# A relative bias tile read back skewed from sixteen copies in DRAM, and a score block taken in front of a chunk's split

## The reference

```python
def t5_bucket(dist):
    d = jnp.maximum(dist, 0)
    large = 16 + (log(max(d, 1) / 16) / log(8) * 16).astype(int32)   # at most 31
    return jnp.where(d < 16, d, large)

# selected and window branches (8 heads), for query t and key s:
s_w = einsum(qb, kb) * scale + head_bias[:, :, t5_bucket(t - s)]
# compressed branch: block n ends at position 16 n + 31, 15 blocks
s_c = einsum(qb, kc) * scale + head_bias[:, :, t5_bucket(t - (16 * n + 31))]
# sliding window of 128 with sinks (4 more heads)
s = einsum(q, k) * scale + head_bias_swa[:, :, t5_bucket(t - s)]
```

## Time and profile before

| | |
|---|---|
| median of three runs | 2382.7 us |
| the profiled execution, its span | 2386.48 us, 2384.7 us |
| mean granted TensorE clock | 0.982 of full speed |
| TensorE busy | 2305.5 us, 97% |
| VectorE busy | 1540.0 us, 65% |
| ScalarE busy | 1187.1 us, 50% |
| GpSimd busy | 66.7 us, 3% |
| DMA, mean over the span | 206 GB/s |

### The profile page before, as it was taken

How to read it: one execution, slowest core, us unless ns; L and a number is a source line. 1 busy time by engine, 2 the same in 40 slices (tenths; PEclk the granted TensorE clock), 3 DMA queues, 4 the chain that set the end, 5 groups by cost and what they waited for, 6 DMA issues and landing times.

```text
span 2384.7 us, 34244 instructions
## 1 busy us (share of the span) xinstructions
PE 2305.5 (97%) x14956; PEld 2068.2 (87%) x14956; DVE 1540.0 (65%) x1425; ACT 1187.1 (50%) x1156; POOL 66.7 (3%) x84
## 2 busy tenths in 40 slices
PE   8999999999999999999999999999999999799998
PEld 8997989799899888897998999778888898688886
DVE  4654655666466547556664666668888566588887
ACT  3433544443343346344433544467776554377774
POOL 1000100000000001000000000000000100000000
PEclk8999999999999999999999999999999999799999
DMA  6554434455555554444655555489998554499995
GB/s 207 182 190 159 144 121 145 153 168 189 183 176 178 193 167 131 141 128 151 196 188 174 177 177 187 143 288 355 357 349 301 174 186 149 143 335 347 343 370 191
DMA packets 309613, 490.92 MB, mean 206 GB/s; under 512 B 15349, under 2 KB 204965, under 8 KB 309457
## 3 DMA queue, kind: packets, MB, share of 16 engines
q1 hardware_dynamic: 305696, 475.35, 59.3%
q0 software_dynamic: 2912, 10.14, 1.3%
q10 hardware_dynamic: 848, 3.15, 0.4%
HBM read 487.53 MB, written 1.07 MB: 205 GB/s over the span
## 4 chain that ended last, share of the span: by engine, by line
PE 90%; DVE 5%; ACT 2%; issue 1%; POOL 0%; DMA 0%; DVEq 0%; ACTq 0%
PE PS L682 27%; PE PS L686 26%; PE PS L683 26%; PE PS L1338 1%; ACT RH L1449 1%; PE PS L904 1%; PE PS L869 1%; DVE RL L1932 1%; PE PS L854 1%; PE PS L1268 1%; DVE HTL L1918 1%; PE PS L1344 1%; DVE X L2273 1%; PE PS L843 1%; PE PS L805 0%
## 5 line engine op out<-in xcount | busy, mean ns | idle before, releaser
L1932 DVE TENSOR_TENSOR RL<-RINGS,RH 128x2048 fp32r<-128x2048 f32 x448 | 1017.6, 2273 | 552.4 <-ACT RH L1449 550.0
L1449 ACT ACTIVATE RH<-RINGS 128x2048 fp32r<-128x2048 f32 x448 | 851.3, 1901 | 787.4 <-PE PS L686 787.1
L682 PE MATMUL PS<-RH,HTH 128*128 128x256 f32 (+1 forms) x1728 | 565.2, 338 | 4.7 <-DVE HTL L1918 2.6
L683 PE MATMUL PS<-RH,HTL 128*128 128x256 f32 (+1 forms) x1728 | 553.3, 331 | 0.0
L682 PE MATMUL PS<-HTH,RH 128*128 128x256 f32 (+1 forms) x1568 | 416.9, 285 | 12.2 <-ACT RH L1449 5.0
L683 PE MATMUL PS<-HTL,RH 128*128 128x256 f32 (+1 forms) x1568 | 413.3, 282 | 0.0
L686 PE MATMUL PS<-RL,HTH 128*128 128x256 f32 (+1 forms) x1728 | 408.1, 328 | 0.0
L682 PEld LDWEIGHTS PS<-RH,HTH 128*128 128x128 f32 x1728 | 330.4, 191 | 40.1 <-issue 5.8
L683 PEld LDWEIGHTS PS<-RH,HTL 128*128 128x128 f32 x1728 | 331.5, 192 | 29.0 <-issue 0.2
L686 PE MATMUL PS<-HTH,RL 128*128 128x256 f32 (+1 forms) x1568 | 329.6, 283 | 1.4 <-DVE RL L1932 1.4
L686 PEld LDWEIGHTS PS<-RL,HTH 128*128 128x128 f32 x1728 | 296.9, 191 | 31.4
(11 more groups left out here) (413 smaller groups left out, 2282.1 us busy)
## 6 DMA issues: line engine op xcount, KB each, us to landing
RINGS<-w_in SPq DMA_DIRECT2D x64, 1024.0 KB, 5.3
RINGS<-w_gate SPq DMA_DIRECT2D x64, 1024.0 KB, 5.4
RINGS<-w_up SPq DMA_DIRECT2D x64, 1024.0 KB, 5.5
RINGS<-w_down SPq DMA_DIRECT2D x64, 1024.0 KB, 5.4
RINGS<-ffn_w_gate SPq DMA_DIRECT2D x44, 1024.0 KB, 5.4
RINGS<-ffn_w_up SPq DMA_DIRECT2D x44, 1024.0 KB, 5.3
RINGS<-ffn_w_down SPq DMA_DIRECT2D x44, 1024.0 KB, 4.9
RINGS<-w_out SPq DMA_DIRECT2D x16, 1024.0 KB, 5.0
```

What stands on the lines that cost most here:

```text
L682: mm(dst, a_[0], b_[0], start=start, stop=False)
L683: mm(dst, a_[0], b_[1], start=False, stop=False) if left else mm(dst, a_[1], b_[0], start=False, stop=False)
L1449: A(splits.buffer(RH, RH3)[:, 0:width], RINGS[:, slot, 0:width], ACT.Copy).then_inc(wh_ready, 1)
L1932: TTn(RL[:, slot, 0:width], RINGS[:, slot, 0:width], splits.buffer(RH, RH3)[:, 0:width].bitcast(F32), ALU.subtract).then_inc(wl_ready, 1)
```

## The change

The one row per head stays. GpSimd now stores it sixteen times in DRAM, as (16, 12, 512). Eight DMAs then read it back, each to 16 partitions. Within one DMA partition p reads from copy p with a shift of p elements back, which gives the right order of partitions at once, directly into BIAS. The flip matmuls, the reversed identity, the matrix HOT with its load, and the 30 matmuls for BIASC go. VectorE adds the masks in place in BIAS, behind the last chunk pair of the first FFN, and in projection step 2 copies every sixteenth element of BIAS into BIASC; blocks that the first 128 rows never see come from the mask. In both layers `softmax(0)` and `blocks(0)` move from the start of step 9 to the end of step 8, in front of that step's `split`, and `blocks(0)` stands between the addition and the maximum of `softmax(0)`.

```diff
-NLOAD = 6
+NLOAD = 5
+COPIES = 16
@@ gpsimd
-            nc.gpsimd.dma_start(HOT, hot).then_inc(consts_loaded, 16)
...
-                    nc.gpsimd.dma_start(scratch, VBIAS).then_inc(bias_stored, 16)
+                    nc.gpsimd.dma_start(scratch.rearrange("r h n -> h r n"), spread(VBIAS, 1, COPIES)).then_inc(bias_stored, 16)
                     pool.wait_ge(bias_stored, 16)
-                    nc.gpsimd.dma_start(BFLIP, bass.AP(tensor=scratch.tensor, offset=P, ap=[[1, P], [512, 12], [1, S]])).then_inc(bias_loaded, 16)
+
+                    for q in range(0, P, COPIES):
+                        nc.gpsimd.dma_start(BIAS[q:q + COPIES, :, :], bass.AP(tensor=scratch.tensor, offset=S - 1 - q,
+                                                                              ap=[[12 * 512 - 1, COPIES], [512, 12], [1, S]])).then_inc(bias_loaded, 16)
@@ tensor
-                    if l + f == 0 and j == 1:
-                        for t in range(T):
-                            for n in range(NCMP):
-                                u = t * P - 16 * n - 31 + 256
-                                last = mm(PS[:, 6, (t * NCMP + n) * 8:(t * NCMP + n + 1) * 8], HOT[:, u:u + P], RB[:, 0:8], start=True, stop=True)
-                        last.then_inc(hot_ready, 1)
                 if l + f == 0:
-                    pe.wait_ge(bias_taken, 4)
+                    pe.wait_ge(bias_row, 1)
...
-                    if l == 0 and j == 0:
-                        pe.wait_ge(bias_loaded, 16)
-                        for b in range(6):
-                            last = mm(PS[:, 4 + b if b < 4 else b - 2, :], CON[:, O_FLIP:O_FLIP + P], BFLIP[:, 2 * b:2 * b + 2, :].rearrange("p h n -> p (h n)"), start=True, stop=True)
-                        last.then_inc(hot_ready, 1)
                     if j == 2:
-                        if l == 0:
-                            pe.wait_ge(bias_taken, 6)
@@ vector, swiglu
+                if l + f == 0:
+                    dve.wait_ge(bias_loaded, 16 * (P // COPIES))
+                    TTn(BIAS[:, 0:8, :], BIAS[:, 0:8, :], spread(CON[:, O_MB:O_MB + S], 1, 8), ALU.add).then_inc(bias_taken, 1)
+                    TTn(BIAS[:, 8:12, :], BIAS[:, 8:12, :], spread(CON[:, O_MS:O_MS + S], 1, 4), ALU.add).then_inc(bias_taken, 1)
                 for j in range(FR - 2):
                     split()
@@ vector, softmax
                     TTn(p.rearrange("p (g j n) -> p g j n", g=2, n=nk), PS[:, 2:4, 0:nj * nk].rearrange("p g (j n) -> p g j n", n=nk),
                         bias, ALU.add).then_inc(sc_taken, 1)
+                    if between is not None:
+                        between()
@@ vector, projection
+                    if l == 0 and i == 2:
                         dve.wait_ge(zeroed, 4)
-                        dve.wait_ge(bias_taken, 6)
+                        dve.wait_ge(bias_taken, 2)
+                        for t in range(T):
+                            seen = 7 if t == 0 else NCMP
+                            first = P + 31 - t * P
+                            for r in range(2):
+                                own = BIASC[:, r * 8 + t * 4:r * 8 + t * 4 + 4, :]
+                                V.tensor_copy(own[:, :, 0:seen].rearrange("p (g i) n -> p g i n", g=2),
+                                              BIAS[:, 0:8, first:first + 16 * seen - 15:16].rearrange("p (g r i) n -> p r g i n", g=2, r=2)[:, r]).then_inc(bias_taken, 1)
+                                if seen < NCMP:
+                                    V.tensor_copy(own[:, :, seen:NCMP], spread(CON[:, O_MCN + seen:O_MCN + NCMP], 1, 4)).then_inc(bias_taken, 1)
+                        dve.wait_ge(bias_taken, 8)
...
                     if i == 9:
-                        softmax(0)
-                        dve.wait_ge(pads_zeroed, l + 1)
-                        dve.wait_ge(ktr_ready, 2 * l + 1)
-                        blocks(0)
                         dve.wait_ge(head_sq, 2 * l + 2)
...
+                    if i == 8:
+
+                        def first_blocks():
+                            dve.wait_ge(pads_zeroed, l + 1)
+                            dve.wait_ge(ktr_ready, 2 * l + 1)
+                            blocks(0)
+
+                        softmax(0, first_blocks)
                     if i <= 10 or i >= 16:
                         split(K * W1[i + 2] if i + 2 < N1 else SLOT)
```

More of the change, by code:

```diff
@@ L206, in loop, with build @@
         c.after(m, count, per)
-def build(nc, a, out, con, hot_rev, hot, vect, scratch):
+def build(nc, a, out, con, hot_rev, vect, scratch):
     ctx = ExitStack()
@@ L290, in build @@
         BT = BTF.rearrange("p (a r n) -> p a r n", a=2, r=16)
-        BFLIP = TT[:, 0:12, :]
-        HOTR, HOT, VBIAS = (TT[0:n, 12 + 2 * i:14 + 2 * i, :].rearrange("p a n -> p (a n)") for i, n in enumerate((32, 32, 12)))
+        HOTR, VBIAS = (TT[0:n, 12 + 2 * i:14 + 2 * i, :].rearrange("p a n -> p (a n)") for i, n in enumerate((32, 12)))
         DIAG = TT[:, 18, :].rearrange("p (t n) -> p t n", t=T)
@@ L1987, in swiglu @@
                         V.tensor_copy(VBIAS, PS[0:12, 5, :]).then_inc(bias_row, 1)
-                    if l + f == 0 and j == 1:
-                        dve.wait_ge(hot_ready, 2)
-                        for t in range(T):
-                            for r in range(2):
-                                TTn(BIASC[:, r * 8 + t * 4:r * 8 + t * 4 + 4, :].rearrange("p (g i) n -> p g i n", g=2),
-                                    PS[:, 6, t * NCMP * 8:(t + 1) * NCMP * 8].rearrange("p (n g r i) -> p r g i n", g=2, r=2, i=2)[:, r],
-                                    spread(spread(CON[:, O_MCN + t * NCMP:O_MCN + (t + 1) * NCMP], 1, 2), 1, 2), ALU.add).then_inc(bias_taken, 1)
+                if l + f == 0:
+                    dve.wait_ge(bias_loaded, 16 * (P // COPIES))
+                    TTn(BIAS[:, 0:8, :], BIAS[:, 0:8, :], spread(CON[:, O_MB:O_MB + S], 1, 8), ALU.add).then_inc(bias_taken, 1)
+                    TTn(BIAS[:, 8:12, :], BIAS[:, 8:12, :], spread(CON[:, O_MS:O_MS + S], 1, 4), ALU.add).then_inc(bias_taken, 1)
                 for j in range(FR - 2):
@@ L2026, in _, with softmax @@
                 heads = PROJ[:, :, NG:NG + 24]
-                def softmax(u):
+                def softmax(u, between=None):
                     kind, t, j0, nj = UNITS[u]
@@ L2101, in _ @@
                         outputs(i - 12)
-                    if l == 0 and i == 1:
-                        dve.wait_ge(hot_ready, 3)
-                        TTn(BIAS[:, 0:8, :], HIGH.rearrange("p (h n) -> p h n", h=8), spread(CON[:, O_MB:O_MB + S], 1, 8), ALU.add).then_inc(bias_taken, 1)
-                        TTn(BIAS[:, 8:12, :], LOW[:, 4 * S:8 * S].rearrange("p (h n) -> p h n", h=4), spread(CON[:, O_MS:O_MS + S], 1, 4), ALU.add).then_inc(bias_taken, 1)
+                    if l == 0 and i == 2:
                         dve.wait_ge(zeroed, 4)
-                        dve.wait_ge(bias_taken, 6)
+                        dve.wait_ge(bias_taken, 2)
[9 more added lines that the diff above has]
+                        dve.wait_ge(bias_taken, 8)
                     if i == 3:
@@ L2670, in constants @@
     hot_rev = (t5_bucket(383 - w) == b).astype(np.float32)
-    hot = (t5_bucket(w - 256) == b).astype(np.float32)
-    return con, hot_rev, hot
+    return con, hot_rev
 def input_order():
@@ L2711 @@
     arrays = {n: np.ascontiguousarray(x) for n, x in inputs.items()}
-    for n, x in zip(("con", "hot_rev", "hot"), constants()):
+    for n, x in zip(("con", "hot_rev"), constants()):
         arrays[n] = x
@@ L2717 @@
     out = nc.dram_tensor("out", (1, S, D), F32, kind="ExternalOutput").ap()
-    scratch = nc.dram_tensor("bias_scratch", (12, 512), F32, kind="Internal").ap()
-    build(nc, aps, out, aps["con"], aps["hot_rev"], aps["hot"], aps["vect"], scratch)
+    scratch = nc.dram_tensor("bias_scratch", (COPIES, 12, 512), F32, kind="Internal").ap()
+    build(nc, aps, out, aps["con"], aps["hot_rev"], aps["vect"], scratch)
     r = run(nc, [arrays], core_ids=[0])
```

7 lines of the change are left out of this document (3 added, 4 removed).

## The result

The changed kernel takes 2367.2 us (median of five runs, 2364.41 to 2373.23) against 2382.7 us before on the same chip: 0.9936 of it, with an interval of 0.9917 to 0.9955. That is 15.5 us faster; the forecast was 18.4 us faster, 2364.3 us, with a range of 2358 to 2370.

What follows compares the result with a forecast made beforehand. TensorE, busy 97% of the span, was taken to bound the kernel. Terms 13.3 + 5.15 + 0 + 0 - 0.1 = 18.4 us, taken from 2382.7, gave 2364.3 us; own range 2361.5 to 2367, wider 2358 to 2370.

Steps and rivals of the forecast that it cites:

- A: First FFN: removing the 60 matmuls for BIASC gives 13.3 us, 10.7 of it matmuls and about 2.5 clock.
- B: Projection, between chunks 0 and 1: removing the six flip matmuls gives 5.15 us, bounds 4.5 and 5.15.
- C: VectorE's new bias additions and six small copies into BIASC fall into its idle time; cost 0, at most 1.3 us.
- D: The 16-fold store and eight reads beside the ring loads in the first FFN: between 0 and 3 us, taken as 0.
- R3: Rival: the eight DMAs are so slow that VectorE waits for them and the kernel gets slower; chance 0.02.
- E: Moved scores and blocks, both layers: scores(2) 4.3 us earlier together, less 4.4 for low clock in new waits; -0.1 us.
- R1: Rival: no clock fall in the new score waits, or in one only; 2359.9 or 2362.1 us; chance 0.20.
- R2: Rival: half clock after 43 us not from the BIASC matmuls, 2366.9 us, or a late ring, 2369.9; chance 0.08.
- R4: Rival: the moved block brings scores(2) no earlier and the clock falls late; 2364.3 to 2366.4 us; worse end's chance 0.08.

Runs made afterwards that it cites:

- undo_move: The changed kernel with the scores of unit 0 and first block tiles put back in front of step 9's work on VectorE; 2367.1 us, ratio 0.9924 to before.
- best: The changed kernel with the edits of early_add and paced together; 2352.1 us, ratio 0.9860 to before.
- before_eight: The kernel before, with its one 128-partition read cut into eight reads of 16 adjacent partitions from the one DRAM copy; 2387.2 us, run once.
- tiny_paced: paced plus 30 unused matmuls (32-row weights, 8 columns) where the BIASC matmuls had been; run once, 11.6 us added between two ring issues there.
- early_add: The changed kernel with unit 1's scores taken from PSUM before the second block tiles and head-row scaling; 2357.8 us, ratio 0.9884 to before.
- paced: The changed kernel with each of the eight bias reads held back until one more first-FFN chunk is computed; 2362.5 us, ratio 0.9911 to before.
- stride8: The changed kernel with each of the eight reads going to partitions 8 apart instead of 16 adjacent ones; 2362.1 us, ratio 0.9898 to before.

## Why the prediction was right, point by point

- **A, 13.3 us: right in sum, wrong in its parts.** It gave 13.3 (13.9 less the 0.7 us that after was ahead by at 40 us; there its clock is 1.00 at 12 to 19 us, while the profiles of before, undo_move and best have 0.50). I called 10.7 us the matmuls and 2.5 clock. But 8.2 of the 10.7 us of the block itself ran at the low clock: at full clock it is 6.4 us, and 6.8 are clock. So the forecast counted a large part of the clock's price as matmuls; the sum is the same, since both go with the block. The lower bound of 10.7 "if the clock fell anyway" was no bound; an estimate from these rows is 6.4. The Trainium skill's rule on idle gaps ("TensorE: Matmul & The Clock Gate", "Why this matters for your kernels") was rightly set aside: the clock fell with TensorE busy throughout in four of five such blocks.
- **B, 5.15: right**, 5.2 measured (15.44 less 10.28 at the ring issues around it).
- **C, 0: right.** The additions filled the idle time before a split, the six copies took 0.7 us ahead of a split that still waited 3.56.
- **D, 0: the term that was mis-sized.** It was taken as 0 and cost 3.7 us in the profiled execution, 5.1 and 6.3 in two more with the same transfers. The step that failed is "the bytes need about 6 us" at 292 GB/s: that rate was read from a read of 128 partitions and put on reads of 16, which moved 141 GB/s in before_eight against 318, and took 17.3 us. The upper bound of 3 us, from the same rate, was too low. The forecast also watched the wrong load, that issued at 40.6 us, and did not ask what part A does to the next one. Before, that was issued at 59.60, when the read had landed (50.4); without the block it is issued at 45.67, into the reads, and takes 16.9 us. I looked for the stall at 45 to 55 us; it came at 64.7, three chunks behind that issue. The wait of VectorE was free, as said, and R3 was never near.
- **E, -0.1: right at the place, in part by luck in the whole.** Scores(2) come 2.5 us earlier in layer 0 and 1.8 in layer 1, as computed; the wait of 4.1 us is there in both layers (4.10 and 4.06), with 3.4 and 6.8 us of low clock. The rows for that price were read short: the stretch called 3.3 us long had begun at 1551.7 us and lasted 6.8, and the low stretches of before in all are 3.4 to 13.7 us long. From the scores to the last FFN of the first stack after loses 0.3 us against before, but undo_move took 5 us less than after there and tiny_paced 6 us less, by the clock alone, so no total shows E to better than that. What early_add adds is that the second score addition stood behind the key blocks and the head rows, and that this order, not the move, set the wait.
- **The sum.** 0.7 at the start + 13.3 + 5.2 - 3.7 - 0.3 = 15.2, the lead that after has in the traces as it enters the second stack; the medians say 15.5. The forecast of 18.4 missed by about 3 us, and D is nearly all of it. That 15.2 and 15.5 agree so well is luck, as the 7 us in the second stack and the spread of the runs show. Of the rivals, R1 did not come, and R2 only with its second half, the ring stall; R4 was wrong in its cause, as scores(2) did come earlier.

## What to carry to other kernels

When a block of matmuls is removed, ask which transfers now meet: the next ring load moved from 59.6 to 45.7 us, into a bulk load that it had followed before. Spread such a bulk load over the chunks with a wait on a counter (paced: no stall), or let each DMA span the partitions (stride8: 0.9 us). When a wait is moved rather than removed, read which instruction releases it and put that one first; here one addition ahead of its neighbours was worth more than moving the whole group. And compare stretches of two traces at full clock as well as in time, since the low stretches alone moved the same work by 5 us.

## What the runs showed of the hardware that was not expected

- Eight reads of 16 adjacent partitions, together 1536 KB, held the DMA engines at a full share and moved 140 and 142 GB/s (before_eight), where one read of 128 partitions moved 318. The ring load issued among them took 16.9, 18.4 and 18.5 us (after, undo_move, early_add); one alone took 5.3.
- The clock of TensorE fell to 0.50 with no idle time recorded within blocks of matmuls of 32 rows by 8 columns, 128 by 8 and 32 by 256, and not in one of 128 by 256. The same is seen in the attention: in after it goes low within a block of 64 rows by 15 columns that starts at 1019.60, with TensorE busy throughout:

```profile
1019.00:1020.00 1.00, 1.00 (x14) 0.93 (x13) 0.00 (x0) 1.00 (x1) 0.00 (x0) 1.00 0.82 198
1020.00:1023.00 3.00, 3.00 (x33) 2.96 (x33) 2.26 (x2) 1.98 (x2) 0.00 (x0) 0.66 0.84 287
```

- Behind a wait of 1.28 us that every kernel has near 465 us (the second FFN in the table) the clock fell in early_add and best and not in after: the same short wait was followed by no loss in one kernel and by one of 1.4 us (the lead of early_add goes from 16.9 to 15.5 us) in another.
